# Compression stage of a hybrid decoder step on one Trainium2 core: page rows turned 64 columns at a time, and split at full width

## The reference, cut to what matters

```
ch = rows.reshape(B, n_chunks, 16, G, D)              # D = 64, G = 2
proj = einsum('bnsgd,psdh->pbngh', ch, w1)            # p = 2 parts, h = 256
h = proj[0][:n_blk] + bias[0] + proj[1][1:n_blk+1] + bias[1]
out = einsum('bngh,hd->bngd', silu(h), w2)
```

## Time and profile before

| | before |
|---|---|
| median of runs | 2283.69 us |
| the profiled execution: its span | 2288.2 us (the only time of it that is on record) |
| PE busy over the span | 2140.2 us, 94% |
| DVE, ACT, POOL busy | 63%, 44%, 27% |
| L3163, its three groups of 512 products | 217.4, 205.2 and 205.1 us busy |
| L3046, x576 / L2929, x576 | 230.5 us / 200.6 us busy |
| mean granted TensorE clock | 0.964 |

### The profile page before, as it was taken

How to read it: one execution, slowest core, us unless ns; L and a number is a source line. 1 busy time by engine, 2 the same in 40 slices (tenths; PEclk the granted TensorE clock), 3 DMA queues, 4 the chain that set the end, 5 groups by cost and what they waited for, 6 DMA issues and landing times. The chain is left out here.

```text
span 2288.2 us, 40887 instructions
## 1 busy us (share of the span) xinstructions
PE 2140.2 (94%) x15798; PEld 1924.4 (84%) x15798; DVE 1437.0 (63%) x3226; ACT 1006.7 (44%) x2204; POOL 607.6 (27%) x937
## 2 busy tenths in 40 slices
PE   6999999999999999976789898988999999999998
PEld 5999997877877787764678786867999999999997
DVE  4212326876876786776487787358786777755643
ACT  4115114554553554444376575224333333355543
POOL 0001103432432342320088594134111111120100
PEclk9999999999999999987889899989999999999999
DMA  4116555754554555469310112211212222285743
GB/s 125 56 56 187 210 194 164 244 172 150 198 172 152 170 189 165 112 156 301 125 54 8 44 47 67 92 63 58 92 57 85 85 73 96 95 275 177 234 155 104
DMA packets 212457, 300.75 MB, mean 131 GB/s; under 512 B 24674, under 2 KB 176546, under 8 KB 202882
## 3 DMA queue, kind: packets, MB, share of 16 engines
q1 hardware_dynamic: 192136, 188.22, 26.5%
q0 software_dynamic: 20128, 109.92, 13.9%
HBM read 231.26 MB, written 73.70 MB: 133 GB/s over the span
## 5 line engine op out<-in xcount | busy, mean ns | idle before, releaser
L3046 DVE TENSOR_TENSOR a_XTL<-cpt,a_XTH 64x256 fp32r<-64x256 f32 (+1 forms) x576 | 230.5, 400 | 62.4 <-ACT a_XTH L2929 54.0
L2929 ACT CAST a_XTH<-cpt 64x256 fp32r<-64x256 f32 (+1 forms) x576 | 200.6, 348 | 106.2 <-PE cpt L3148 94.9
L3163 PE MATMUL cph<-a_XTH,w1H 128*128 128x512 f32 x512 | 217.4, 425 | 0.0
L3163 PE MATMUL cph<-a_XTL,w1H 128*128 128x512 f32 x512 | 205.2, 401 | 0.0
L3163 PE MATMUL cph<-a_XTH,w1L 128*128 128x512 f32 x512 | 205.1, 401 | 0.0
L1955 PE MATMUL f<-a_aH,wdH 128*128 128x352 f32 x528 | 172.3, 326 | 0.0
L1797 DVE TENSOR_TENSOR wdL<-raw,wdH 128x512 fp32r<-128x512 f32 x132 | 91.2, 692 | 128.8 <-ACT wdH L1630 128.3
L1955 PE MATMUL f<-a_aH,wdL 128*128 128x352 f32 x528 | 170.9, 324 | 0.0
L1507 POOL TENSOR_TENSOR C<-C,a_mt 128x264 f32<-128x264 f32 x66 | 68.3, 1055 | 368.8 <-ACT C L1622 241.7
L1914 PE MATMUL f<-a_b,ring 128*128 128x264 f32 x1056 | 142.5, 284 | 3.9 <-DVE a_b L1738 3.3
L1630 ACT CAST wdH<-raw 128x512 fp32r<-128x512 f32 x132 | 81.5, 618 | 131.9 <-PE f L1955 111.4
(11 more groups left out here) (556 smaller groups left out, 5888.9 us busy)
## 6 DMA issues: line engine op xcount, KB each, us to landing
raw<-in_w_down SPq DMA_DIRECT2D x132, 256.0 KB, 2.9
raw<-in_w_in POOLq DMA_DIRECT2D x12, 1024.0 KB
a_V<-v_s SPq DMA_DIRECT2D x6, 2048.0 KB, 15.1
v_s<-X SPq DMA_DIRECT2D x22, 512.0 KB, 6.4
raw<-in_w_gate SPq DMA_DIRECT2D x11, 1024.0 KB, 6.3
raw_odd<-in_w_val SPq DMA_DIRECT2D x11, 1024.0 KB, 6.2
a_T<-C SPq DMA_DIRECT2D x20, 528.0 KB, 3.2
z_tok<-stage SPq DMA_DIRECT2D x48, 128.0 KB
```

Of the source, the lines that this page charges most:

```text
L2929: nc.scalar.copy(turned(XTH, u, s, k, g, a), split(bank(at, k)[:], u, k, g, a)).then_inc(h_ready, 1)
L3046: last = nc.vector.tensor_tensor(turned(XTL, u, s, k, g, a), split(bank(at, k)[:], u, k, g, a), hi.bitcast(F32), ALU.subtract)
L3163: last = nc.tensor.matmul(out[:, :, 0:n], w[:, s, k, q, m * P:(m + 1) * P], x[:, s % 2, k, :, q:q + n], **flags)
```

## The change: what it does

Kinds 0 and 1 are no longer turned by a transpose of all 128 columns. Every 64 columns of one head and one token are the stationary operand of an ordinary float32 product with the identity, and its result is written to partition half a. The loops run over head i, chunk half h and token a: eight products of 128 rows, 64 stationary columns and 128 moving columns in place of four transposes (for the prompt four products of 64 rows, 64 stationary and 64 moving columns in place of two transposes). The bank then has the layout of `XTH`: partition = (token, d), column = (head, chunk). One copy and one subtraction of 128 x 512 (128 x 128 for the prompt) make the high and the low part. Kind 2 is turned as before, and the order of the calls on all queues stays.

```diff
-        def split(src, u, k, g, a):
-            ...
+        def landed(src, u):
+            return src.rearrange("p (g n) -> p g n", g=NG) if u < DB else src[:, 0:NG * NCP]
 
-        def turned(X2, u, s, k, g, a):
-            ...
+        def turned(X2, u, s, k):
+            if u == DB:
+                return X2[:, s % 2, k].rearrange("p g n -> p (g n)")[:, 0:NG * NCP]
+            return X2[:, s % 2, k, :, 0:256]
...
-                for g in range(NG):
-                    for a in range(2):
-                        nc.scalar.copy(turned(XTH, u, s, k, g, a), split(bank(at, k)[:], u, k, g, a)).then_inc(h_ready, 1)
+                nc.scalar.copy(turned(XTH, u, s, k), landed(bank(at, k)[:], u)).then_inc(h_ready, 1)
...
-                for g in range(NG):
-                    dve.wait_ge(h_ready, 8 * at + 4 * k + 2 * g + 2)
-                    for a in range(2):
-                        ...
-                last.then_inc(l_ready, 1)
+                dve.wait_ge(h_ready, 2 * at + k + 1)
+                nc.vector.tensor_tensor(turned(XTL, u, s, k), landed(bank(at, k)[:], u), turned(XTH, u, s, k).bitcast(F32), ALU.subtract
+                                        ).then_inc(l_ready, 1)
...
-                for h in range(2 if u < DB else 1):
-                    for a in range(2):
-                        c = P * (2 * h + a if kind < 2 else 2 * a + h)
-                        src = X[j % 3][0:r, h, 2 * (s % 2) + a] if u < DB else XP[0:r, j - TILES, 2 * (s % 2) + a]
-                        last = nc.tensor.transpose(bank(at, kind)[:, c:c + r], src[:, P * kind:P * kind + P], ident[0:r, 0:r])
+                t0 = 2 * (s % 2)
+                for i in range(2):
+                    for h in range(2 if u < DB else 1):
+                        src = X[j % 3][0:r, h, t0:t0 + 2] if u < DB else XP[0:r, j - TILES, t0:t0 + 2]
+                        if kind == 2:
+                            c = P * (2 * i + h)
+                            last = nc.tensor.transpose(bank(at, kind)[:, c:c + r], src[:, i, 2 * P:3 * P], ident[0:r, 0:r])
+                            continue
+                        c = P * (2 * i + h) if u < DB else r * i
+                        for a in range(2):
+                            last = nc.tensor.matmul(bank(at, kind)[DK * a:DK * a + DK, c:c + r], src[:, a, P * kind + DK * i:P * kind + DK * i + DK],
+                                                    ident[0:r, 0:r], start=True, stop=True)
                 last.then_inc(t_ready[kind], 1)
```

More of the change, by code:

```diff
@@ L2617, in rows @@
             return P if u < DB else NCP
-        def split(src, u, k, g, a):
-            r = rows(u)
-            s4 = src.rearrange("p (h a c) -> p h a c", h=2, a=2)[DK * g:DK * g + DK]
-            return s4[:, :, a, :] if u < DB else s4[:, 0, a, 0:r]
-        def turned(X2, u, s, k, g, a):
+        def landed(src, u):
+            return src.rearrange("p (g n) -> p g n", g=NG) if u < DB else src[:, 0:NG * NCP]
+        def turned(X2, u, s, k):
             if u == DB:
-                return X2[DK * a:DK * a + DK, s % 2, k].rearrange("p g n -> p (g n)")[:, NCP * g:NCP * g + NCP]
-            dst = X2[DK * a:DK * a + DK, s % 2, k, g, :]
-            return dst[:, 0:256].rearrange("p (h c) -> p h c", h=2)
+                return X2[:, s % 2, k].rearrange("p g n -> p (g n)")[:, 0:NG * NCP]
+            return X2[:, s % 2, k, :, 0:256]
         LAST = NS * NU
@@ L3041, in low_parts @@
                 u, s = at // NS, at % NS
-                for g in range(NG):
-                    dve.wait_ge(h_ready, 8 * at + 4 * k + 2 * g + 2)
-                    for a in range(2):
-                        hi = turned(XTH, u, s, k, g, a)
-                        last = nc.vector.tensor_tensor(turned(XTL, u, s, k, g, a), split(bank(at, k)[:], u, k, g, a), hi.bitcast(F32), ALU.subtract)
-                last.then_inc(l_ready, 1)
+                dve.wait_ge(h_ready, 2 * at + k + 1)
+                nc.vector.tensor_tensor(turned(XTL, u, s, k), landed(bank(at, k)[:], u), turned(XTH, u, s, k).bitcast(F32), ALU.subtract
+                                        ).then_inc(l_ready, 1)
             def keys(at):
```

## The result

The changed kernel takes 2363.55 us (median of 4 runs, 2359.81 to 2371.72), the one before 2284.82 us beside it (4 runs, 2278.14 to 2293.02). That is 79 us slower, where 2363 us and +79 us were forecast. The ratio on record is 1.0336, with a 95% interval of 1.0301 to 1.0371, or 69 to 85 us. (The ratios here are those on record; the quotient of two medians can differ from them by up to 0.002.)

The account below looks back on a forecast made before the run. TensorE was taken to bound the sequences until 970 us, with waits for DVE in the prompt's steps. +84 (sequences) + 1 - 6 (prompt) = +79 us on 2283.7 gives 2363 us, range 2340 to 2400.

Parts of the forecast that it names:

- TensorE paces the sequences, nothing else does: Until 970 us only TensorE's time counts (PE busy 561.5 of 570 us); cheaper ACT and DVE work gains nothing there.
- A product is two records of 0.11, two halves side by side, price as the row of `blocks`: In `turn`, eight products are 16 records; the partition halves overlap, so they take 0.87 us, 1.15 with shape changes.
- Seams 0.28, so 0.72 a bundle, 0.44 ahead of `wide_products`: Sequences: changing the array's shape costs 0.28 us; 100 bundles at 0.72 more and 28 at 0.44 give 84 us.
- The decode chunks' waits stay: In the sequences, PE's waits of 3.9 and 2.5 us for DVE's small operations in the scan were left unchanged.
- The prompt: -6 + 1: Prompt's steps: 5 us of waits and 1 of clock given back, 1 us added for dearer products.
- The waits: Prompt's steps: of PE's 8.0 us of waits for DVE, the shorter split gives back 5.
- The bundle: Prompt's `turn`: four products take 0.49 us against 0.45 for two transposes; 16 x 0.04 = 0.6 us, called 1.
- the clock, for which I counted 1: Prompt's steps: the lowered granted clock cost about 3 us; with smaller gaps 1 us of it comes back.
- The lower bound: Sequences: if changes of the array's shape cost 0.1 us instead of 0.28, the cost is 128 x 0.18 = 23 us less.
- Rival A: In the new bundles the two halves work one behind the other: +194 us, 2478 us; chance 0.10.

Follow-up runs that it names:

- narrow-split twin: The changed kernel's 64-column products, but with four copies and four subtractions of 64 x 256 for each bank as before: 2372.61 us, ratio 1.0383.
- full-split kernel: The kernel before with its transposes kept and the change's full-width copy and subtraction, rearrangement of heads and tokens left out: 2276.72 us, ratio 0.9951.
- both bundles together: The changed kernel with turn(at+1, 0) moved behind project(at, 0), right ahead of turn(at+1, 1): 2352.14 us, ratio 1.0271.

## Why the prediction was right

By its own steps:

- *TensorE paces the sequences, nothing else does.* Right, and shown from both sides: the products alone bring the whole +83 us there, the full-width split alone changes 605.9 to 605.2.
- *A product is two records of 0.11, two halves side by side, price as the row of `blocks`.* Right. The 1.02 us from the bundle to the next product came out to the hundredth, and halving the columns halved the stream.
- *Seams 0.28, so 0.72 a bundle, 0.44 ahead of `wide_products`.* 0.06 too small and right. An ordinary bundle costs 0.78. The stream is 8 x 0.109 = 0.87, so the seams are 0.34: 0.09 ahead, 0.15 in the 1.02, and 0.10 in the two products behind, of which I had counted 0.04 (the distance of the two is 0.34 instead of 0.23; behind transposes it was 0.31 already, so part of it was there before too). The bundles are 100 x 0.78 + 28 x 0.43 = 90 us instead of 84.
- *The decode chunks' waits stay.* Right to the tenth. What I had left out beside them is the clock. Before, it falls in three stretches within the sequences, behind the three decode chunks; in the changed kernel one is left (the row of 955 to 965 above). The windows of the kernel before:

```profile
536.00:546.00 10.00, 9.27 (x54) 6.91 (x55) 7.29 (x31) 2.94 (x8) 0.00 (x0) 0.83 0.01 2
706.00:716.00 10.00, 8.69 (x21) 5.13 (x20) 6.83 (x29) 2.31 (x8) 0.00 (x0) 0.66 0.08 29
884.00:894.00 10.00, 9.10 (x53) 6.81 (x54) 7.46 (x31) 2.94 (x8) 0.00 (x0) 0.83 0.01 2
```

  0.17, 0.34 and 0.17 of ten microseconds are 6.8 us of work lost; after it is 3.4. With the 1.6 us that `blocks` no longer waits for `a_sx`, 90 - 3.4 - 1.6 = 85, where the trace has 82.9 + 3.2 = 86. So 84 was nearly right because a price 6 us too low and 5 us of small gains that were not counted cancel.
- *The prompt: -6 + 1.* Right in sign, and 2 us too small: -7.1 in the trace, and by the medians 7 to 9 us between the changed kernel and its narrow-split twin and 10 between the full-width split on the transposes and the kernel before. Term by term it is less good. The waits gave 4.3 where I counted 5. The bundle costs 0.11 more, not 0.04: the changed and the full-split kernel's bundles of the prompt lie that far apart, 2 us over 16. And the clock, for which I counted 1, is worth up to 5. Whether the full-width split is what keeps it up was not settled. It was 0.88 over the prompt's steps in both traces with the narrow split; in the eight with the full-width one it was 1.00 in six, but 0.95 with both bundles together and 0.87 with the transposes.
- *The lower bound* has a slip: seams are charged only in 100 bundles, so with seams of 0.1 us the sum falls by 100 x 0.18 = 18 us and not by 23.
- *Rival A* (the halves do not overlap) names a real mechanism that this order avoids; it appears when the order gives it room, and then with half of its price: 58 of the 115 us by which A's 2478 lies above the forecast.
- The select stage and what follows is 3.3 us longer in the profiled execution after than before. Nothing there was changed, and the executions of one kernel differ by more (2359.81 to 2371.72).

So the mechanism is shown and was forecast, but that the sum meets the measured difference to the microsecond is luck: the forecast has 2 us too little cost in the sequences and 2 us too little gain behind them, and the interval of the measured difference is 16 us wide.

## What to carry to other kernels

Ask which engine the stage waits for before making another one's work cheaper: here 1 us saved on ACT and DVE for every bank was worth nothing where TensorE was full, and about 0.5 us a bank where it waited (7 to 10 us over the prompt's 16), the clock included. Price a new form of instruction by the row of the trace with the same shape and the same length of stream, seams included, rather than by parts. If a layout is to be changed, look for the place that is free: the prompt's rows could be laid out by the DMA that brings them, and that gave the prompt's gain with the transposes left as they were.

## What the runs showed of the hardware

- Two products of 64 stationary columns into the two partition halves of one PSUM bank ran side by side, two records per 0.109 us at 128 moving columns and about 0.058 at 64 ((1.02 - 0.61) / 8 = 0.051 less).
- The overlap reaches across the queue's order for groups of four records (+0.06 us a bundle) but not for eight (+0.49, with four records running alone at either end).
- Going into the shape 128*64 and back cost 0.34 us in all (this includes the 0.08 us by which the second product behind a bundle of transposes came late as well). Between two bundles of the same shape it cost nothing: the second added 0.87 us.
- In this kernel the granted clock fell behind the decode chunks' gaps of 1.3 us three times before and once after, with the same gaps, and in the other kernels once to three times. Why behind one and not behind another was not settled; in the sequences it moved single traces by 3 us, in the prompt's steps by 5.
